# A layer norm over channel tiles with one mean product each, and the next stage's first weights prepared in it

## The chip, the cores and the metric
One core of a Trainium2 chip (trn2) runs the whole program: one launch, five engines (TensorE or PE, VectorE or DVE, ScalarE or ACT, GpSimd or POOL, and SyncE or SP, which issues transfers) and 16 DMA engines. The metric is the device time of one execution in microseconds, as the median of several runs.

## The reference
A layer of a diffusion backbone on 2048 tokens of 1024 channels, with 256 context tokens. What bears on the change:

```python
def conv_module(proj, taps, bias, ln_g, ln_b, conv_fn):
    u = proj[..., OFF_CONV_A:OFF_CONV_B] * jax.nn.sigmoid(proj[..., OFF_CONV_B:OFF_Q])
    u = conv_fn(u, taps) + bias
    return jax.nn.silu(layernorm(u, ln_g, ln_b))
...
def forget_gate(f_logits, lb):
    f = lb + (1.0 - lb) * jax.nn.sigmoid(f_logits.astype(jnp.float32))
    return split_heads(jnp.log(f)), split_heads(1.0 - f)
...
    lower_bounds = jnp.cumsum(jax.nn.softmax(hgrn_lb_logits, axis=0), axis=0)[:DEPTH]
```

One input projection (`w_in`, 3584 columns) feeds the convolution (columns A and B), the four heads of a gated recurrence (q, v, two forget gates FF and FB, output gate g). Convolution and heads are joined, projected out and gated; then comes a routed mixture of 16 experts, and a last norm.

## The kernel before, in words
The program is a row of stages, each with its own block of engine programs and its own scope `cleanup_on_exit`, which frees the stage's memory, clears its semaphores on GpSimd and ends in a barrier: `modulate_stage` (L96), `conv_stage` (L364), `heads_stage` (L739), `outproj_stage` (L1541), `topk_stage`, `moe_stage`. A further such scope, `front` (L2493), stands around the first two and holds `ConvWeights`, the four staging slabs `wst` for 128 columns of `w_in` each. Float32 weights are split into a bf16 high part (ScalarE casts) and a bf16 low part (VectorE subtracts), and every projection is three bf16 products (`triple`, L89 to L91), 24 instructions for a 512-token tile.

`conv_stage`. Channels lie on the partitions in four tiles (NCT = 4), tokens in four segments of 512 (NSEG = 4). PE makes the pairs A and B for each channel tile and segment (`pa`, `pb`, two banks each, with the semaphore `u_ok` giving the bank back); ScalarE takes the tanh (L506), VectorE the product `u` (`gated`, L579), then 31 taps per channel tile into `co` (L592, L607). POOL first issues the parameters (taps, bias `cb`, norm `lg`, then `adab`), and VectorE waits for `par_in` ahead of its first `gated` (L573).

Between its own work PE does *jobs* in a fixed order `KIND`: 18 for v, 32 for q and g, and four small ones, "mod", which sum the products of `modulation`. Each job is written to one of four PSUM banks `pjob`; ScalarE copies it into `jb` (L496, two buffers) and POOL stores it (L474). Twelve jobs lie beside the pairs, 17 beside the taps, and `LN_JOBS` spreads the others over the four segments of the layer norm, with the last two in `REST`.

The layer norm, for each segment n: PE multiplies `co` by a constant matrix of 1/512 for each of the four channel tiles into `pmu` (`mean`, L715); VectorE subtracts (`centre`, L625); ScalarE squares into one of two buffers `sq` (L525); PE multiplies each by the same matrix into `pva` (L728); ScalarE takes the root (L534), VectorE the reciprocal (L644) and scales (L648); then for each channel tile ScalarE scale and bias (L549), tanh (L552), VectorE the product (L659), ScalarE a bf16 cast (L541), VectorE the low part (L654), and SP stores both. After every second channel tile VectorE makes one `modulation` sum (L633, L636), eight instructions of 256 elements, from rows that SP has loaded into the place of `u`. `mean(n + 1)` is issued ahead of segment n's variance.

`heads_stage`. For each head, ten units of up to 512 tokens alternate in direction. A unit's gate: PE projects with `whi`, `wlo` (`project`, L1431), ScalarE takes the tanh (L1065), VectorE makes f with the constants `gh` and `gb` (L1237), POOL makes k = 1 - f (`keep`, L997), ScalarE the log, VectorE the running sum with `segm` (L1247), ScalarE the exponentials (L1081, L1083), POOL the decayed k into the block matrix `KX` and `KK` (`decay_k`, L1006 to L1013), PE its transposes (L1441), and so on. The stage starts with the loads of the norm's scale `ng` and the bound logits `lbr` (SP L902, L903, POOL L977), the first head's weights (L909), cast (L1057) and subtracted (L1225), and `lbd`, `gh`, `gb` (L1214 to L1218, L1052). POOL makes the masks `segm` and `msk` first, and clears `AT` and `KX` (L1029 to L1031) after two `keep`.

## Time and profile before

| what | value |
|---|---|
| median of 3 runs | 2456.59 us (2454.57 to 2457.14) |
| the profiled execution's own time | 2455.54 us |
| its span, first to last instruction | 2453.8 us |
| mean granted clock of TensorE | 0.957 of full speed |

The profile is of one execution. A row of the timeline is: start in us, duration in us, engine, line, operation, output tile <- input tiles, form, count, and in brackets the idle time of the engine before it with what ended it. PE rows of neighbouring matmuls overlap: each shows its whole way through the array, while the next starts before it ends. DMA rows on SP and POOL show the issue, not the transfer.

### The profile page before, as it was taken

The numbers are of one execution on the slowest core, as the hardware profiler recorded it, in microseconds if no ns is written. First come the engines' busy times: TensorE is split into PE (matmuls) and PEld (weight loads), VectorE is DVE, ScalarE is ACT, GpSimd is POOL, SyncE is SP. The second block draws the span as 40 slices with busy tenths as digits, with TensorE's granted clock in tenths as the row PEclk, the third lists the DMA queues.
The fourth block names the chain that finished last, engine by engine and source line by source line (L and its number), as shares of the span: only waits on it lengthen the run. The fifth ranks groups of instructions, "written<-read, shape, count | busy, mean of one in ns | idle before, by whom it ended". The sixth has DMA issues, their size and how long they took to land. (4 is left out here: it accounts for less than half of the span.)

```text
span 2453.8 us, 38986 instructions
## 1 busy us (share of the span) xinstructions
PE 2256.4 (92%) x14964; PEld 1514.2 (62%) x14964; DVE 1565.2 (64%) x2251; ACT 1039.6 (42%) x1333; POOL 547.9 (22%) x572
## 2 busy tenths in 40 slices
PE   7799999996999898979994699999999999999995
PEld 3344444433777786845552477777777777777773
DVE  2759998554668686843334566666666666666666
ACT  3511011443555656544442244444444444444445
POOL 1600001002546464603334111111110111111111
PEclk9799999998999999979996799999999999999998
DMA  8431013344011111334445376777667677676676
GB/s 325 83 78 35 18 30 109 97 142 127 8 48 42 48 41 30 119 104 151 144 155 210 129 240 218 230 234 230 225 220 231 217 234 225 221 239 226 220 248 257
DMA packets 220978, 379.51 MB, mean 155 GB/s; under 512 B 43970, under 2 KB 81986, under 8 KB 220363
## 3 DMA queue, kind: packets, MB, share of 16 engines
q1 hardware_dynamic: 202620, 319.22, 39.1%
q0 software_dynamic: 16656, 56.99, 8.6%
q10 hardware_dynamic: 1616, 2.16, 0.3%
q8 instruction: 53, 0.87, 0.2%
q14 instruction: 33, 0.27, 0.0%
HBM read 314.62 MB, written 63.72 MB: 154 GB/s over the span
## 5 line engine op out<-in xcount | busy, mean ns | idle before, releaser
L89 PE MATMUL pgu<-xhi,mwhi 128*128 128x256 bf16 x2048 | 559.6, 273 | 0.8 <-DVE xlo L2288 0.8
L91 PE MATMUL pgu<-xhi,mwlo 128*128 128x256 bf16 x2048 | 559.6, 273 | 0.0
L90 PE MATMUL pgu<-xlo,mwhi 128*128 128x256 bf16 x2048 | 559.5, 273 | 0.0
L2293 DVE TENSOR_TENSOR mwlo<-mwst,mwhi 128x2048 bf16<-128x2048 f32 x187 | 426.9, 2283 | 0.0
L2197 ACT ACTIVATE mwhi<-mwst 128x2048 bf16<-128x2048 f32 x186 | 350.8, 1902 | 0.0
L2205 ACT ACTIVATE thb<-pgu 128x256 f32<-128x256 f32 x128 | 49.1, 384 | 550.9 <-PE pgu L91 550.9
L607 DVE SCALAR_TENSOR_TENSOR co<-u,taps,co 128x1984 f32<-128x1984 f32 (+22 forms) x120 | 234.1, 1951 | 3.7
L2137 POOL TENSOR_TENSOR mpflag<-mpflag 1x1 f32<-1x1 f32 x46 | 37.2, 808 | 855.6 <-DVE ysb L2320 579.1
L2304 DVE SCALAR_TENSOR_TENSOR thb<-thb,pgu 128x256 f32<-128x256 f32 x128 | 53.8, 420 | 261.7 <-ACT thb L2205 261.7
L89 PEld LDWEIGHTS pgu<-xhi,mwhi 128*128 128x128 bf16 x2048 | 200.8, 98 | 26.1 <-DVE xlo L2288 1.1
L90 PEld LDWEIGHTS pgu<-xlo,mwhi 128*128 128x128 bf16 x2048 | 200.8, 98 | 24.9
L91 PEld LDWEIGHTS pgu<-xhi,mwlo 128*128 128x128 bf16 x2048 | 200.8, 98 | 23.6
L2445 PE MATMUL pd<-mwhi,fhi 128*128 128x512 bf16 x512 | 194.8, 381 | 4.2 <-DVE ysb L2320 3.0
L2447 PE MATMUL pd<-mwhi,flo 128*128 128x512 bf16 x512 | 194.7, 380 | 0.0
L2446 PE MATMUL pd<-mwlo,fhi 128*128 128x512 bf16 x512 | 194.7, 380 | 0.0
L1453 PEld LDWEIGHTS pat<-E,KX 128*128 128x128 f32 x1024 | 150.2, 194 | 23.3 <-POOL KX L1013 8.5
L1431 PE MATMUL pj<-hhi,hwhi 128*128 128x512 bf16 (+1 forms) x320 | 118.4, 370 | 46.1 <-DVE hwlo L1225 27.5
L1453 PE MATMUL pat<-E,KX 128*128 128x32 f32 x1024 | 143.8, 251 | 11.1 <-POOL KX L1013 6.3
L1431 PE MATMUL pj<-hlo,hwhi 128*128 128x512 bf16 (+1 forms) x320 | 118.1, 369 | 0.0
L1431 PE MATMUL pj<-hhi,hwlo 128*128 128x512 bf16 (+1 forms) x320 | 117.5, 367 | 0.0
L496 ACT ACTIVATE jb<-pjob 128x512 f32<-128x512 f32 (+1 forms) x54 | 31.6, 594 | 172.7 <-PE pjob L91 149.8
L2320 DVE SCALAR_TENSOR_TENSOR ysb<-pd,gate,g 128x512 f32<-128x512 f32 x64 | 47.9, 749 | 84.5 <-PE pd L2447 84.5
(352 smaller groups left out, 4426.9 us busy)
## 6 DMA issues: line engine op xcount, KB each, us to landing
mwst<-in_w_gate SPq DMA_DIRECT2D x32, 2048.0 KB, 8.9
mwst<-in_w_up SPq DMA_DIRECT2D x32, 2048.0 KB, 7.9
mwst<-in_w_down SPq DMA_DIRECT2D x32, 2048.0 KB, 7.9
big<-in_ada_w SPq DMA_DIRECT2D x5, 2048.0 KB, 13.1
wst<-in_w_in SPq DMA_DIRECT2D x20, 512.0 KB, 4.9
s_rows<-row SPq DMA_DIRECT2D x16, 520.0 KB, 2.9
u<-in_ada_w SPq DMA_DIRECT2D x8, 1024.0 KB, 6.4
xt<-in_x SPq DMA_DIRECT2D x16, 512.0 KB, 4.4
```

Of the source, the lines that this page charges most:

```text
L89: nc.tensor.matmul(out, lh, rh, start=(k == 0), stop=False)
L90: nc.tensor.matmul(out, lh, rl, start=False, stop=False)
L91: last = nc.tensor.matmul(out, ll, rh, start=False, stop=(k == n - 1))
L607: nc.vector.scalar_tensor_tensor(o, i, taps[:, c, k:k + 1], o, ALU.mult, ALU.add).then_inc(tap_ok, 1)
L1431: ins = nc.tensor.matmul(pj[:, 0:n], w, x, start=(mm == 0), stop=(mm == 3 * KD - 1))
L1453: ins = nc.tensor.matmul(pat[:, n * CH:(n + 1) * CH], KX[:, p, n * P:(n + 1) * P], E[:, p, n * CH:(n + 1) * CH], start=True, stop=True)
L2197: nc.scalar.activation(whi[:, b, ks], wst[:, b % NS, ks], ACT.Copy).then_inc(w_hi, 1)
L2293: nc.vector.tensor_tensor(wlo[:, b, ks], wst[:, b % NS, ks], whi[:, b, ks], ALU.subtract)\
L2304: nc.vector.scalar_tensor_tensor(thb[:, p], thb[:, p], 1.0, pgu[p][:, 0, :], ALU.add, ALU.mult)\
L2445: nc.tensor.matmul(pd[q % 2][:], fh, whi[:, 4 + c, k, :], start=(k == 0), stop=False)
L2446: nc.tensor.matmul(pd[q % 2][:], fh, wlo[:, 4 + c, k, :], start=False, stop=False)
L2447: last = nc.tensor.matmul(pd[q % 2][:], fl, whi[:, 4 + c, k, :], start=False, stop=(k == KD - 1))
```

## The change
It has three parts.

In the conv stage's layer norm VectorE sums the four channel tiles (`channel_sum`, into the free buffer `th`) and the four squares (`square_sum`, in `sq`, now four buffers), in two adds each, and PE makes one product for the mean and one for the variance. The order of jobs around them is new: one before `mean(n + 1)`, one before the variance; the "mod" job is second in its group. `modulation` has one buffer `msum` and other places in VectorE's order; PE's wait for all the taps goes. The squares of the next segment are made right after the root. The last three jobs are stored by SP, with semaphores `late_out` of their own.

A class `GateWeights`, allocated for the whole mixer, holds weights, parameters and bounds of the heads. It uses the four slabs of `wst` (two for staging, one each for high and low). The conv stage loads the first head's two weight blocks, casts and subtracts them in segment 0, queues the parameters on POOL behind the conv stage's, and makes `lbd`, `gh`, `gb`, `ng`. The scope `front` is gone; its tiles live in the mixer's scope.

The heads stage starts with `load(0)` on SP; its loads of `ng` and `lbr`, `load_w(0)`, and the first head's casts, subtractions and bounds are removed; POOL clears `KX[:, 0]` ahead of `msk`, VectorE clears `KX[:, 1]` and `AT` at its start.

```diff
+class GateWeights:
+    def __init__(self, m, I, st):
+        self.st = st[:, 0:2]
+        self.hi = st[:, 2].rearrange("p k n -> p (k n)").bitcast(BF16).rearrange("p (d k n) -> p d k n", d=2, k=KD)
+        self.lo = st[:, 3].rearrange("p k n -> p (k n)").bitcast(BF16).rearrange("p (d k n) -> p d k n", d=2, k=KD)
...
+    def load(self, sp, h, d):
+        col = (COL_FF, COL_FB)[d]
+        sp.dma_start(self.st[:, d], self.src[:, :, bass.ds(h * P + col, P)]).then_inc(self.loaded[d], 16)
...
-            KIND.insert(first + WITH_LN, ("mod", n - 1))
+            KIND.insert(first + 1, ("mod", n - 1))
-    KIND.append(("mod", NSEG - 1))
+    KIND.insert(-1, ("mod", NSEG - 1))
...
@@ SP, conv stage @@
                 load_ada(0)
                 load_ada(1)
+                sp.wait_ge(w_lo, len(SLAB))
+                for d in range(2):
+                    GW_.load(sp, 0, d)
                 for n in range(NSEG):
                     for c in range(NCT):
                         q = n * NCT + c
+                        if c in (0, 2) and n + 1 < NSEG:
+                            e = 2 * n + c // 2
+                            sp.wait_ge(ada_ok, KD * (e + 1))
+                            load_ada(e + 2)
                         sp.wait_ge(ml_ok, q + 1)
...
-                        if q % 2 == 1 and q // 2 + 2 < 2 * NSEG:
-                            sp.wait_ge(ada_ok, KD * (q // 2 + 1))
-                            load_ada(q // 2 + 2)
+                for j in LATE:
+                    sp.wait_ge(job_ok, j + 1)
+                    sp.dma_start(*to_store(j)).then_inc(late_out[j % 2], 16)
...
@@ POOL, conv stage, after adab @@
+                    pool.dma_start(GW_.ng[:], I["hgrn_norm_g"][0].rearrange("(h p) -> p h", p=P)).then_inc(GW_.par_in, 16)
+                    for l in range(2):
+                        for d in range(2):
+                            pool.dma_start(GW_.lbr[:, l, d, :], I["hgrn_lb_logits"][l, d].rearrange("(h p) -> p h", p=P))\
+                                .then_inc(GW_.par_in, 16)
...
@@ ScalarE, conv stage @@
+                nc.scalar.activation(GW_.lbd[:], GW_.lbd[:], ACT.Tanh, scale=0.5).then_inc(GW_.lb_ok, 1)
+                squares(0)
                 for n in range(NSEG):
...
+                    job(LN_JOBS[n][0])
+                    act.wait_ge(va_ps, n + 1)
...
                     job(LN_JOBS[n][1])
+                    if n + 1 < NSEG:
+                        squares(n + 1)
+                    job(LN_JOBS[n][2])
+                    if n == 0:
+                        for d in range(2):
+                            act.wait_ge(GW_.loaded[d], 16)
+                            nc.scalar.activation(GW_.hi[:, d], GW_.st[:, d], ACT.Copy).then_inc(GW_.hi_ok, 1)
...
@@ VectorE, conv stage @@
                 nc.vector.tensor_scalar(lg[:], lg[:], 0.5, None, ALU.mult).then_inc(par_ok, 1)
+                dve.wait_ge(GW_.par_in, 80)
+                nc.vector.tensor_tensor(GW_.lbd[:], GW_.lbr[:, 0], GW_.lbr[:, 1], ALU.subtract).then_inc(GW_.lb_ok, 1)
+                nc.vector.tensor_scalar(GW_.ng[:], GW_.ng[:], 0.5, None, ALU.mult).then_inc(GW_.lb_ok, 1)
...
+                def channel_sum(n):
+                    if n >= 1:
+                        dve.wait_ge(mu_ps, n)
+                    x = co[:, :, n * SEG:(n + 1) * SEG]
+                    nc.vector.tensor_tensor(th[:], x[:, 0:2], x[:, 2:4], ALU.add).then_inc(sx_ok, 1)
+                    dve.wait_ge(sx_ok, 2 * n + 1)
+                    nc.vector.tensor_tensor(th[:, 0], th[:, 0], th[:, 1], ALU.add).then_inc(sx_ok, 1)
+                def square_sum(n):
+                    dve.wait_ge(sq_ok, NCT * (n + 1))
+                    nc.vector.tensor_tensor(sq[:, 0:2], sq[:, 0:2], sq[:, 2:4], ALU.add).then_inc(ss_ok, 1)
+                    dve.wait_ge(ss_ok, 2 * n + 1)
+                    nc.vector.tensor_tensor(sq[:, 0], sq[:, 0], sq[:, 1], ALU.add).then_inc(ss_ok, 1)
...
+                channel_sum(0)
                 centre(0)
+                channel_sum(1)
+                square_sum(0)
...
                 for n in range(NSEG):
                     if n + 1 < NSEG:
                         centre(n + 1)
+                    if n + 2 < NSEG:
+                        channel_sum(n + 2)
+                    modulation(2 * n)
+                    if n == NSEG - 1:
+                        modulation(2 * n + 1)
...
+                    if n + 1 < NSEG:
+                        square_sum(n + 1)
...
-                        if c % 2 == 1:
-                            modulation(q // 2)
+                        if c == 1 and n < NSEG - 1:
+                            modulation(2 * n + 1)
                     low(n * NCT + NCT - 1)
+                    if n == 0:
+                        for d in range(2):
+                            dve.wait_ge(GW_.hi_ok, d + 1)
+                            nc.vector.tensor_tensor(GW_.lo[:, d], GW_.st[:, d], GW_.hi[:, d], ALU.subtract)\
+                                .then_inc(GW_.lo_ok, 1)
...
@@ PE, conv stage @@
-                pe.wait_ge(tap_ok, NCT * TAPS)
...
-                    for c in range(NCT):
-                        last = nc.tensor.matmul(pmu[n % 2][:], K["mean_cw"][:], co[:, c, n * SEG:(n + 1) * SEG],
+                    pe.wait_ge(sx_ok, 2 * n + 2)
+                    nc.tensor.matmul(pmu[n % 2][:], K["mean_cw"][:], th[:, 0], start=True, stop=True).then_inc(mu_ps, 1)
                 mean(0)
                 for n in range(NSEG):
+                    job(LN_JOBS[n][0])
                     if n + 1 < NSEG:
                         mean(n + 1)
+                    job(LN_JOBS[n][1])
...
+                    pe.wait_ge(ss_ok, 2 * n + 2)
+                    nc.tensor.matmul(pva[n % 2][:], K["mean_cw"][:], sq[:, 0], start=True, stop=True).then_inc(va_ps, 1)
+                    for j in LN_JOBS[n][2:]:
                         job(j)
...
@@ heads stage @@
-                load_w(0)
...
@@ POOL, heads stage @@
                 nc.gpsimd.memset(segm[:], 1.0).then_inc(msk_ok, 1)
+                nc.gpsimd.memset(pflag[:], 0.0).then_inc(pf_ok, 1)
+                wait(pool, msk_ok, 1)
+                nc.gpsimd.memset(segm[:, 0:SEG:P], 0.0).then_inc(msk_ok, 1)
+                nc.gpsimd.memset(KX[:, 0], 0.0).then_inc(zero_ok, 1)
                 nc.gpsimd.memset(msk[:], 1.0).then_inc(msk_ok, 1)
...
@@ VectorE, heads stage @@
-                wait(dve, msk_ok, 5)
+                nc.vector.memset(KX[:, 1], 0.0).then_inc(at0_ok, 1)
+                nc.vector.memset(AT[:], 0.0).then_inc(at0_ok, 1)
...
@@ build @@
-            with nc.cleanup_on_exit(), ExitStack() as front:
-                CW_ = ConvWeights(Mem(nc, front), I)
-                modulate_stage(nc, K, I, scr, CW_)
-                conv_stage(nc, K, I, scr, CW_)
+            CW_ = ConvWeights(mm, I)
+            GW_ = GateWeights(mm, I, CW_.st)
+            modulate_stage(nc, K, I, scr, CW_)
+            conv_stage(nc, K, I, scr, CW_, GW_)
```

## Rows read from the trace of the kernel before

**Rows 1.** The page: busy time of the engines.
```profile
PE 2256.4 (92%) x14964; PEld 1514.2 (62%) x14964; DVE 1565.2 (64%) x2251; ACT 1039.6 (42%) x1333; POOL 547.9 (22%) x572
```

**Rows 2.** Busy time by stretch: microseconds, engines (busy, count), PEclk, DMA share, GB/s.
```profile
120.00:431.00 311.00, 311.00 (x1442) 141.05 (x1441) 266.40 (x158) 41.52 (x60) 22.78 (x32) 1.00 0.20 56
431.00:581.00 150.00, 145.61 (x586) 61.38 (x584) 82.92 (x132) 67.28 (x102) 13.51 (x26) 1.00 0.37 110
581.00:600.00 19.00, 0.39 (x2) 0.28 (x3) 2.37 (x10) 2.10 (x3) 5.50 (x10) 0.53 0.52 137
```

**Rows 3.** Timeline, first PE matmul of heads: start, us, idle before.
```profile
599.62 0.39 PE L1431 MATMUL pj<-hhi,hwhi 128*128 128x256 bf16 x1 [19.54 <-DVE hwlo L1225]
```

**Rows 4.** Groups by line, 431 to 581 us: count, busy us, mean ns, idle before.
```profile
L728 PE MATMUL pb<-sq,mean_cw 128*128 128x512 f32 x32 | 16.2, 609 | 3.5 <-ACT sq L525 3.5
...
L715 PE MATMUL pa<-co,mean_cw 128*128 128x512 f32 x32 | 14.3, 596 | 0.0
L644 DVE RECIPROCAL rs<-rs 128x512 f32<-128x512 f32 x4 | 13.4, 3353 | 34.0 <-ACT rs L534 34.0
...
L659 DVE SCALAR_TENSOR_TENSOR y<-tl,y 128x512 f32<-128x512 f32 x16 | 11.0, 690 | 16.1 <-ACT tl L552 16.1
```

**Rows 5.** Timeline in the layer norm, ACT, PE and VectorE.
```profile
426.07 0.60 ACT L496 ACTIVATE jb<-pjob 128x512 f32<-128x512 f32 x1 [4.58 <-PE pjob L91]
...
431.05 7.03 PE L715 MATMUL pa<-co,mean_cw 128*128 128x512 f32 x16
...
434.76 2.48 DVE L625 TENSOR_TENSOR co<-co,pa 128x512 f32<-128x512 f32 x4 [12.92 <-PE pa L715]
...
492.14 3.61 DVE L636 SCALAR_TENSOR_TENSOR msum<-u,sil,msum 128x256 f32<-128x256 f32 x7
```

**Rows 6.** Timeline at the end of the conv stage, PE, POOL and SP.
```profile
579.06 1.01 PE L683 MATMUL pjob<-adab,ident 4*1 4x512 f32 x2
...
580.99 0.51 POOL L474 DMA_DIRECT2D s_modrows<-jb  x1 [1.30 <-ACT jb L496]
...
588.87 0.39 SPq L902 DMA_DIRECT2D ng<-in_hgrn_norm_g  x1
```

**Rows 7.** Timeline of the parameters of the conv stage, POOL, VectorE, ScalarE.
```profile
129.08 0.78 POOL L458 DMA_DIRECT2D cb<-in_conv_bias  x1 [12.96 <-issue]
...
130.59 0.75 POOL L460 DMA_DIRECT2D lg<-in_conv_ln_b  x1
...
133.21 0.23 DVE L573 TENSOR_SCALAR taps<-taps 128x124 f32<-128x124 f32 x1 [18.83 <-DMA lg<-in_conv_ln_b]
...
134.01 1.22 DVE L568 TENSOR_TENSOR wlo<-wst,whi 128x1024 bf16<-128x1024 f32 x1
...
136.00 0.60 ACT L506 ACTIVATE th<-pb 128x512 f32<-128x512 f32 x1 [7.37 <-PE pb L91]
```

**Rows 8.** Stores: issues by tile with median us to landing; SP's timeline.
```profile
s_modrows<-jb POOLq DMA_DIRECT2D x1, 2.0 KB, 1.6
...
s_mixed<-ml SPq DMA_DIRECT2D x5, 128.0 KB, 2.0
...
1070.51 2.09 SPq L964 DMA_DIRECT2D s_mixed<-KX  x4
1075.63 0.56 SPq L1608 DMA_DIRECT2D hhi<-s_mixed  x1
```

**Rows 9.** Timeline of the first units of the heads stage, POOL, VectorE, PE.
```profile
611.45 1.79 POOL L1031 MEMSET KX<- 128x2048 f32 x1
613.33 1.01 POOL L1006 TENSOR_TENSOR KX<-KK,B 128x256 f32<-128x256 f32 x1
...
610.68 2.59 DVE L1254 COPY sm<-B 128x8 f32<-128x8 f32 x1
...
615.09 0.44 PE L1441 MATMUL pk<-ident,KK 128*128 128x128 f32 x2 [1.83 <-POOL KK L1009]
```

More of the change, by code:

```diff
@@ L899, in _ @@
             def _(sp):
-                with nc.allow_non_contiguous_dma(reason="per-channel constants into columns"):
-                    sp.dma_start(ng[:], I["hgrn_norm_g"][0].rearrange("(h p) -> p h", p=P)).then_inc(m_out[0], 16)
-                    sp.dma_start(lbr[:, 0, 0, :], I["hgrn_lb_logits"][0, 0].rearrange("(h p) -> p h", p=P))\
-                        .then_inc(m_out[1], 16)
                 def load_w(h):
-                    for d, col in enumerate((COL_FF, COL_FB)):
+                    for d in range(2):
                         wait(sp, w_lo, h * 2 - 1 + d)
-                        sp.dma_start(wst[:, d], wv[:, :, bass.ds(h * P + col, P)]).then_inc(w_in[d], 16)
+                        GW_.load(sp, h, d)
                 def load(h):
@@ L1049, in _ @@
             def _(act):
-                wait(act, lb_ok, 1)
-                nc.scalar.activation(lbd[:], lbd[:], ACT.Tanh, scale=0.5).then_inc(lb_ok, 1)
                 def split(h, d):
@@ L1349, in _ @@
                     constants(0, d)
[L1350 removed]
                 forget(0, 0)
+                wait(dve, msk_ok, 2)
                 sums(0, 0)
```

168 lines of the change are left out of this document (70 added, 98 removed).

## The prediction

> **What bounds the kernel now.** I read the page first, for the shares of the engines; then the busy time of each engine in chosen stretches; then TensorE's waits and the groups of instructions in the layer norm; last the timeline at the places that the diff touches.
>
> TensorE is busy for 92% of the span [rows 1]. The stretches say more [rows 2]. From 120 to 431 us (projections on PE, the taps on VectorE) PE is busy for all of the 311 us: a microsecond taken from or added to PE is one of the kernel, and VectorE only has to deliver in time. From 431 to 581 us (the layer norm, with q and g projections between) PE has 145.61 of 150 us, VectorE 82.92, ScalarE 67.28: again PE. From 581 to 600 us PE has 0.39 us of work: one stage ends and the next starts, and nothing hides it. The largest wait of PE there is for `hwlo`, the low half of the first head's gate weights, 19.5 us at a time [rows 3]. Nothing behind the heads stage is touched, so what is won ahead of it should reach the end whole.
>
> I measure against the profiled execution: 2455.54 us, span 2453.8 us. The median of the runs shown is 2456.59 us, 1.05 us above it; I add that at the end. 0.2%, 4.9 us, is about what a measurement of this kernel can tell from no change.
>
> **Part 1: the mean products.** Before, each segment has four float32 products for the mean and four for the variance, two instructions each: 32 on L715 and 32 on L728 [rows 4]. The first 16 run in 7.03 us, the last one's drain of 0.6 included, so one starts every 0.43 us [rows 5]. The change leaves a quarter, 16 instructions. PE loses 48 x 0.43 = 20.6 us.
>
> With them go stalls. PE's stretch of the layer norm runs from 430.8 us (just ahead of the first L715, [rows 5]) to 580.07 us (the end of the last L683, [rows 6]): 149.2 us. By the code it holds 21 projection jobs; their pitch is that between two of ScalarE's copies, 4.58 idle + 0.60 = 5.18 us [rows 5], together 108.8. Four modulation jobs are two pairs of instructions, 1.0 us each pair [rows 6]: 8.0. The 64 products: 27.5. The rest, 149.2 - 144.3 = 4.9 us, is waiting; 3.5 us of it are for the squares [rows 4]. Afterwards a job stands between each product and what it needs, so I let 1 us remain: 3.9 us gained. Bounds: none, or all 4.9.
>
> Does VectorE keep up? A middle segment holds: the centring, 2.48; the modulation sums twice, 3.61 for seven instructions of eight, so 4.0 each [rows 5]; the reciprocal, 3.35 [rows 4]; four scalings of the centring's form, 2.5; four of L659 and four splits of the same size at 0.69 [rows 4], 5.5. That is 21.8 us. New are two pairs of adds. The first add of a pair has 1024 elements and two inputs; the nearest row is the 1024-element subtraction of 1.22 us [rows 7]; the second has 512, 0.68. Two pairs: 3.8 us, together 25.6 us. Of the waits for the tanh 16.1 us over 16 stay, 4 us a segment at most [rows 4]; the sums cover some, I allow 3. So VectorE needs 28.6 us a segment and PE 5 x 5.18 + 2.0 + 4 x 0.43 = 29.6 us. It is close, but PE stays the bound, and VectorE starts ahead: it idles 12.92 us until the first mean [rows 5]. In the last segment both modulation sums come ahead of the reciprocal, 8 us, but centring and channel adds are gone there; by this count VectorE ends some 8 us before PE. The second modulation sum of a segment is needed by the second job of the next; walking both queues it is there about 4 us early each time. ScalarE has slack of half the stretch. The stores of the last three jobs move from POOL to SP, behind the `mixed` stores, which are out when VectorE ends. `load_ada` moves ahead of a store on SP and comes earlier.
>
> **Part 2: the parameters.** The norm's scale and the logits, five transfers of 512 four-byte elements, are now queued on POOL at the start of the conv stage, behind `adab`, and VectorE waits for all of them ahead of its first `gated`. POOL issues `cb` and `lg` 0.75 us apart, the last `lg` at 130.59; it has landed at 133.2 us, 2.6 us later, when VectorE starts [rows 7]. With `adab` and five more at 0.75 the last issue is at 135.1 us, landed at 137.7. With 0.2 us of small operations and 0.68 for L579, the first `u` is there at 138.6 us. PE needs it for its third pair of products; ScalarE's tanh of the second comes at 136.00 us [rows 7], and PE's first instruction of the third would be 0.2 us ahead of that. Cost: 138.6 - 135.8 = 2.8 us, on the path, since PE has no idle time from there on. Behind VectorE's wait are the splits of the slabs, which nobody needs so soon. Bounds: nothing, or a landing twice as long, 5.4 us.
>
> PE's end of the stage: 580.07 - 20.6 - 3.9 + 2.8 = 558.4 us.
>
> **Part 3: the end of the stage.** Before, the last store is issued at 580.99, lands 1.6 us later, and SP's first instruction of the next stage is at 588.87, 6.3 us after that [rows 6, 8]. Two clean-ups stand in that gap, of the conv stage and of the scope `front`; the change takes the second away. From the heads to the output projection there is one: the last of four stores is issued at 1072.1 us, lands 2 us later, and the next stage begins at 1075.63 [rows 8], a gap of 1.5 us. So a clean-up is worth nothing to 4.8 us. I take a gap of 3.0 us, nearer to the boundary with the same number. The last store is now of 256 KB on SP instead of 2 KB: SP's of 128 KB land in 2.0 us [rows 8]; I take 2.5, bounds 2 and 4. Next stage: 558.4 + 0.9 + 2.5 + 3.0 = 564.8 us, 24.1 us earlier.
>
> **Part 4: the first head's weights.** Before, PE's first product comes at 599.62 us, 10.75 us after SP's first instruction [rows 3, 6]: load, cast, subtraction. These now stand in the conv stage: two loads on SP while it has nothing else, two casts on ScalarE, two subtractions of 1.22 us [rows 7] on VectorE in the first segment, covered by its lead; without the lead they would cost 2.4 us. PE starts about 0.7 us after SP: gain 10.0 us.
>
> **Part 5: the memsets.** Before, POOL clears `AT` and `KX` between `keep` and `decay_k`; the last takes 1.79 us and `decay_k` starts when it ends, at 613.33 [rows 9]. Now POOL clears half of `KX` ahead and VectorE the rest, while PE projects its first 24 products: POOL has 1.8 us for `KX` and, by that rate, 1.4 for the two others, and the masks, some 5 us, about what PE, ScalarE and VectorE need before `keep`. What PE gains is not the memsets' time but its own wait for `KK`, 1.83 us [rows 9]; next late is PE's own third projection, which ends then. Gain 1.8 us, bounds 0 and 4.
>
> VectorE's copy into `sm` took 2.59 us here, ending with POOL's last memset [rows 9]. The Trainium skill ("SBUF — State Buffer", its part on which ports contend) says that VectorE and GpSimd share a port pair by an exclusive lock held for a whole instruction; the trace agrees. If VectorE's new memsets took that lock too, which no row shows, POOL would be done some 3 us later: part 5 would be worth nothing, its lower bound.
>
> **The sum.** 24.1 + 10.0 + 1.8 = 35.9 us. 2455.54 - 35.9 = 2419.6 us; for the median 2420.7 us.
>
> **The rivals.**
> (a) The gap keeps its 6.3 us, because the start of this stage costs it and not the second clean-up. Against: the boundary at 1075 us. 2420.7 + 3.3 = 2424.0 us. Chance 15%.
> (b) VectorE becomes the bound of the layer norm. For it: 1 us of slack in a segment. With the adds or waits 2 us longer PE waits for sums or variances, 4 to 8 us in all: 2425 to 2429 us. Against: VectorE's lead. Chance 12%.
> (c) POOL's queue stalls once more. It idled 12.96 us ahead of `cb` [rows 7], behind the taps. If the added transfers meet that limit once, the parameters come 13 us later, and PE stands: 2434 us. Against: three of the same size went out 0.75 us apart. Chance 5%.
> (d) Slower, at the same place: every added transfer meets the stall, 5 x 12.96 = 65 us, and PE, without cover, loses it: 2486 us. It decides from the point where the last logits land 36 us later than I say, after 173 us. Chance 2%.
> (e) The change doesn't do what it says: the wait at 599 us comes back as another, for `v`, `q` or the masks, and 10 us less are gained: 2431 us. Against: the first product with `v` comes behind the transposes, which start at 615.09 us [rows 9]. Chance 4%.
>
> **How the numbers follow.** The forecast gets 62%, with a range of its own from 2414 to 2425 us: below, a clean-up worth 1.5 us more, no delay of the parameters (2.8), all stalls gone (1); above, 4 us of terms lost. (a) and (b) reach to 2429 us; so the range is 2412 to 2430 us and leaves out (c), (d), (e) and a rest. Faster by over 0.2%: 0.97, all but (d) and a rest; within 0.01; slower 0.02.
>
> **What would show it.** L715 and L728 with eight instructions each; VectorE's first `u` at 138.6 us; PE's layer norm about 124.7 us long instead of 149.2 and 2.8 us later in its start; 5.5 us from the last store's issue to the next stage, and PE's first product within 1 us of it; no wait for `KK` at the first transposes. PE waits of over 4 us for sums in the layer norm, a pause near 136 us of over 6 us, or a next stage that starts after 570 us would prove me wrong.

## The result and the profile after

The changed kernel takes 2415.24 us, the median of 4 runs (2414.21 to 2418.06), beside 2456.86 us for the kernel before on the same chip: a ratio of 0.9833, with a 95% interval of 0.9816 to 0.9850. The forecast was 2420.7 us in a range of 2412 to 2430. The gain by medians is 41.6 us; between the two profiled executions it is 2453.8 - 2411.7 = 42.1 us of span, where the steps of the forecast add up to 35.9. So the direction and the places were right and 6.2 us are to be accounted for.

The page of the changed kernel, busy time of the engines, beside [rows 1]:

```profile
PE 2220.3 (92%) x14770; PEld 1503.6 (62%) x14916; DVE 1578.7 (65%) x2269; ACT 1038.9 (43%) x1333; POOL 544.5 (23%) x569
```

The weight loads (PEld) are 48 fewer, the number of products taken out; PE's own count is 194 lower, so some 146 of its records are missing here, and its 36.1 us less must not be read as work saved. The stretches below and the timeline are the surer guide. VectorE has 13.5 us more. Busy time by stretch, changed kernel (columns as in [rows 2]):

```profile
120.00:430.80 310.80, 308.06 (x1413) 139.99 (x1432) 268.38 (x162) 41.45 (x60) 26.45 (x37) 1.00 0.20 55
430.80:555.00 124.20, 123.67 (x528) 52.65 (x536) 97.98 (x150) 68.14 (x104) 12.37 (x23) 1.00 0.47 139
555.00:560.00 5.00, 0.76 (x6) 0.57 (x6) 0.23 (x1) 0.60 (x1) 0.70 (x4) 0.97 0.14 53
```

The layer norm is a stretch of 124 us in which PE stands still for half a microsecond; the 19 us of nothing between the stages, 581 to 600 before, are 4.2 us. New is the first line: PE lacks 2.7 us of 310.8 (a part of it missing records), where it had lacked none.

Groups by line in the layer norm, 430.8 to 555 us, changed kernel (columns as in [rows 4]):

```profile
L717 DVE RECIPROCAL rs<-rs 128x512 f32<-128x512 f32 x4 | 13.4, 3348 | 1.3 <-ACT rs L572 1.3
...
L734 DVE SCALAR_TENSOR_TENSOR y<-tl,y 128x512 f32<-128x512 f32 x16 | 10.9, 690 | 10.6 <-ACT tl L597 10.6
...
L679 DVE TENSOR_TENSOR sq<-sq 128x1024 f32<-128x1024 f32 x4 | 4.9, 1219 | 0.0
L805 PE MATMUL pb<-sq,mean_cw 128*128 128x512 f32 x8 | 4.4, 631 | 0.0
L794 PE MATMUL pa<-th,mean_cw 128*128 128x512 f32 x8 | 4.1, 592 | 0.0
...
L673 DVE TENSOR_TENSOR th<-co 128x1024 f32<-128x1024 f32 x3 | 3.7, 1218 | 0.0
```

32 and 32 product instructions are 8 and 8, and neither waits any more (L728 waited 3.5 us before [rows 4]). An add of 1024 elements takes 1.22 us, the row that the forecast took for it; VectorE's wait of 34.0 us for the root [rows 4] is 1.3 us, since the order of the work gives it something else to do meanwhile.

The timeline of the parameters, changed kernel, POOL's and then VectorE's and PE's rows:

```profile
126.38 0.78 POOL L499 DMA_DIRECT2D cb<-in_conv_bias  x1 [11.91 <-issue]
...
129.18 0.80 POOL L504 DMA_DIRECT2D ng<-in_hgrn_norm_g  x1
129.95 3.00 POOL L507 DMA_DIRECT2D lbr<-in_hgrn_lb_logits  x4
...
131.45 0.23 DVE L618 TENSOR_SCALAR taps<-taps 128x124 f32<-128x124 f32 x1 [18.71 <-DMA lg<-in_conv_ln_b]
...
134.83 0.17 DVE L621 TENSOR_TENSOR lbd<-lbr 128x8 f32<-128x8 f32 x1 [3.07 <-DMA lbr<-in_hgrn_lb_logits]
...
135.72 0.39 PE L89 MATMUL pa<-hhi,whi 128*128 128x512 bf16 x1 [1.64 <-DVE u L627]
```

The five transfers go out some 0.75 us apart and no second stall of POOL follows them: rivals (c) and (d) did not come. VectorE waits 3.07 us for the logits, and PE then 1.64 us for VectorE. The cost is read against the first product of the convolution, and in this profile its record is missing, as the weight loads show (the first PE record is of L90, the second product):

```profile
110.52 0.10 PEld L89 LDWEIGHTS pa<-hhi,whi 128*128 128x128 bf16 x1 [8.93 <-DVE wlo L613]
...
110.93 0.63 PE L90 MATMUL pa<-hlo,whi 128*128 128x512 bf16 x1 [9.09 <-DVE wlo L613]
```

So the first product started at 110.53 us, where it was 112.16 before. From there the first mean product comes 318.89 us later before and 320.46 after: the parameters cost 1.6 us, the length of the pause.

The timeline at the end of the conv stage, changed kernel: VectorE's last instruction, ScalarE, SP and the next stage's first rows (beside [rows 3, 6, 9]):

```profile
549.85 0.69 DVE L729 TENSOR_TENSOR ml<-y,mh 128x512 bf16<-128x512 f32 x1 [0.45 <-ACT mh L586]
...
549.73 1.07 ACT L535 ACTIVATE jb<-pjob 128x512 f32<-128x512 f32 x2
553.88 0.59 ACT L535 ACTIVATE jb<-pjob 1x512 f32<-1x512 f32 x1 [3.09 <-DMA s_g<-jb]
555.11 0.60 ACT L535 ACTIVATE jb<-pjob 128x512 f32<-128x512 f32 x1 [0.64 <-PE pjob L91]
...
555.73 0.36 SPq L487 DMA_DIRECT2D s_g<-jb  x1
559.27 0.35 SPq L978 DMA_DIRECT2D v<-s_v  x1
...
559.31 0.27 PE L1472 MATMUL pj<-hhi,wst 128*128 128x256 bf16 x1 [4.24 <-PEq L406]
...
559.77 1.76 DVE L1260 MEMSET KX<- 128x2048 f32 x1 [9.23 <-PEq L406]
559.89 1.81 POOL L1038 MEMSET KX<- 128x2048 f32 x1
...
572.92 0.38 PE L1482 MATMUL pk<-ident,KK 128*128 128x128 f32 x2
```

From the last store's issue to the next stage 3.54 us pass, where it was 7.88 [rows 6]; PE's first product comes 0.04 us behind SP's first instruction, where it was 10.75; and the transposes at 572.92 us wait for nothing, where they waited 1.83 us [rows 9].

### The profile page after: what moved, and what is told of

Same layout as the page of the kernel before. It is cut to its first block and busy times, and to the rows that moved or that the text cites. A ratio compares the mean times of both kernels' runs of the same rounds, so it can differ in the third digit from the quotient of the medians.

```text
span 2411.7 us, 38747 instructions
## 1 busy us (share of the span) xinstructions
PE 2220.3 (92%) x14770; PEld 1503.6 (62%) x14916; DVE 1578.7 (65%) x2269; ACT 1038.9 (43%) x1333; POOL 544.5 (23%) x569
## 5 line engine op out<-in xcount | busy, mean ns | idle before, releaser
L90 PE MATMUL pgu<-xlo,mwhi 128*128 128x256 bf16 x2048 | 559.1, 273 | 0.0
L1472 PE MATMUL pj<-hhi,wst 128*128 128x512 bf16 (+1 forms) x606 | 210.3, 370 | 28.9 <-ACT G L1116 16.2
L90 PEld LDWEIGHTS pgu<-xlo,mwhi 128*128 128x128 bf16 x2048 | 200.7, 98 | 24.8
L2487 PE MATMUL pd<-mwlo,fhi 128*128 128x512 bf16 x497 | 189.1, 381 | 2.9 <-DVE flo L2353 1.4
L2486 PE MATMUL pd<-mwhi,fhi 128*128 128x512 bf16 x481 | 182.9, 380 | 3.3 <-DVE ysb L2361 3.0
L1472 PEld LDWEIGHTS pj<-hhi,wst 128*128 128x128 bf16 x640 | 82.7, 129 | 52.5 <-issue 25.1
L1472 PE MATMUL pj<-hlo,wst 128*128 128x512 bf16 (+1 forms) x310 | 114.2, 368 | 0.9 <-ACT G L1116 0.9
L89 PE MATMUL pjob<-hhi,whi 128*128 128x512 bf16 x251 | 95.1, 379 | 0.3
```

The costliest lines, as they stand in the source:

```text
L89: nc.tensor.matmul(out, lh, rh, start=(k == 0), stop=False)
L90: nc.tensor.matmul(out, lh, rl, start=False, stop=False)
L1472: ins = nc.tensor.matmul(pj[:, 0:n], w, x, start=(mm == 0), stop=(mm == 3 * KD - 1))
L2486: nc.tensor.matmul(pd[q % 2][:], fh, whi[:, 4 + c, k, :], start=(k == 0), stop=False)
L2487: nc.tensor.matmul(pd[q % 2][:], fh, wlo[:, 4 + c, k, :], start=False, stop=False)
```

## The experiments

One execution of a kernel differs from the next by some us (2413.16 to 2417.81 for the changed kernel in after_again), so where a kernel ran once I compare stages of its trace and not its total. These are the marks, all in us. *Taps*: from the convolution's first product to the first mean product. In five profiles (before_again, changed, pool_last and the two with `tail` in the name) the record of that first product is missing; there I count from 0.40 us ahead of the second, the distance that the other nine show. *Norm*: from there to ScalarE's last copy of a job, less the 0.04 us between a job's end and its copy; PE does the whole of it without a pause, unless said. *Gap*: from the last store's issue to SP's first instruction of the heads stage. *First*: from there to PE's first product. *Transposes*: from that product to the first transposes.

| kernel | median (runs) | taps | norm | gap | first | transposes |
|---|---|---|---|---|---|---|
| before | 2456.86 (4) | 318.9 | 149.0 | 7.9 | 10.75 | 15.5 |
| changed | 2415.24 (4) | 320.5 | 124.1 | 3.5 | 0.04 | 13.6 |
| before_again | 2453.48 (1) | 318.6 | 149.3 | 7.9 | 10.7 | 15.2 |
| after_again | 2415.50 (5) | 322.5 | 124.1 | 3.5 | 0.04 | 14.3 |
| scope | 2416.52 (1) | 320.7 | 124.1 | 3.9 | 0.04 | 13.5 |
| pool_last | 2421.27 (1) | 320.7 | 124.1 | 8.3 | 0.04 | 14.5 |
| weights_back | 2422.74 (1) | 322.6 | 124.1 | 3.5 | 6.2 | 14.5 |
| four | 2435.31 (1) | 320.6 | 144.7 | 3.5 | 0.04 | 13.6 |
| memsets | 2417.73 (1) | 320.6 | 124.1 | 3.5 | 0.04 | 15.6 |
| late_par | 2414.15 (5) | 318.9 | 124.1 | 3.5 | 0.04 | 14.4 |
| vector_3us | 2420.30 (1) | 320.4 | 130.4 | 3.5 | 0.05 | 13.9 |
| vector_7us | 2433.95 (1) | 320.6 | 144.0 | 3.5 | 0.04 | 14.0 |
| vector_3us_tail | 2423.78 (1) | 323.1 | 128.0 | 4.8 | 0.04 | 13.4 |
| late_par_tail | 2414.75 (5) | 318.6 | 124.1 | 3.5 | 0.04 | 14.5 |

**Both kernels once more, unchanged**, for how far a profile can be trusted.

> The kernel before once more. Five profiles of the changed kernel and its variants have PE's first product of the conv stage at 110.3 to 112.3 us, the one of before has it at 112.16. If the stage ahead merely strays, this one lies in the same band and PE's first product to the first mean product is 318.9 us again; the gap from the last store's issue to the heads stage is again near 7.9 us.

> The changed kernel once more, to see how far one execution's stages stray. The forecast and the trace differ by 6.2 us: 1.6 us lie ahead of the conv stage, in code that is the same. If that is a matter of the execution, this profile puts PE's first product of the conv stage anywhere between 110.9 and 112.2 us and the rest of the stages keep their lengths to 0.3 us. If the change does it, it comes at 110.9 us again. Median near 2415 us.

The ratio of after_again is 0.9838 (0.9824 to 0.9851). Norm and gap repeat within 0.3 us in both kernels. What does not repeat is the beginning: the convolution's first product comes between 110.3 and 112.3 us in all the profiles, whatever the kernel (110.33 in after_again, outside the band that I expected), and the taps in the changed kernel took 320.5 us in one execution and 322.5 in the other. The second of these has its reason in late_par, below.

**scope: a second clean-up around the first two stages again.**

```diff
-            modulate_stage(nc, K, I, scr, CW_)
-            conv_stage(nc, K, I, scr, CW_, GW_)
+            with nc.cleanup_on_exit():
+                for i in range(4):
+                    nc.alloc_semaphore(f"spare{i}")
+                modulate_stage(nc, K, I, scr, CW_)
+                conv_stage(nc, K, I, scr, CW_, GW_)
```

> Changed kernel with a second clean-up scope around the first two stages, with four semaphores in it, as the kernel before had. Theory A (the second clean-up is what made the gap long): from the last store's issue to SP's first instruction of the heads stage 3.5 us becomes some 8 us, and the span grows by 4 to 5 us. Theory B (rival a: something in the start of this stage cost it): the gap stays within 0.5 us of 3.5 us and the span as it is.

SP's timeline in scope:

```profile
556.52 0.36 SPq L487 DMA_DIRECT2D s_g<-jb  x1
560.45 0.35 SPq L978 DMA_DIRECT2D v<-s_v  x1
```

The gap is 3.93 us against 3.54. A second clean-up with its barrier costs 0.4 us here, where SP issues the last stores. The forecast had given it 3.3 of the 6.3 us, so the gap had another cause, and there was one more thing that the change had altered there: which queue issues the last three stores.

**pool_last: the last three jobs stored by POOL again.**

```diff
-                for j in LATE:
-                    sp.wait_ge(job_ok, j + 1)
-                    sp.dma_start(*to_store(j)).then_inc(late_out[j % 2], 16)
...
-                for j in range(LATE[0]):
+                for j in range(JOBS):
```

> Changed kernel with the last three jobs stored by POOL, as before the change, and not by SP. The run with a second clean-up scope had a gap of 3.93 us against 3.54, so the scope is worth 0.4 us and the 4.4 us by which the gap fell are open. Theory A (it is the stores: POOL's last store, with its clean-up behind it on the same engine, holds the barrier): the gap from the last store's issue to SP's first instruction of heads is 7 to 8 us and the span 4 us longer. Theory B (it is what else went from the boundary): 3.5 us plus 0.7 for a slower landing at most.

Timeline of SP and of POOL at the end of the stage, pool_last:

```profile
564.82 0.36 SPq L971 DMA_DIRECT2D v<-s_v  x1
...
556.51 0.56 POOL L506 DMA_DIRECT2D s_g<-jb  x1 [0.79 <-ACT jb L528]
564.82 0.52 POOL L1027 MEMSET segm<- 128x512 f32 x1 [7.75 <-POOLq L406]
```

A gap of 8.3 us with a single clean-up. The store itself is hardly slower: it lands 2.7 us after its issue, SP's last one in the changed kernel after 2.4 us. So 5.6 us lie between the landing and the next stage where POOL has issued the last store and 1.1 us where SP has. In the kernel before, with POOL's store and two clean-ups, they were 6.3 us, so with POOL as the issuer too the second clean-up is worth at most 0.7 us. What POOL does in the 5.6 us no row shows; its idle time is put down to its own sequencer. The Trainium skill ("DMA: Bandwidth & Descriptors", its first table) gives a transfer from GpSimd about 1 us to its first byte and one from SyncE 0.6 us. By that estimate the store would cost 0.4 us more from POOL; the run says 4.8 us, only 0.3 of it on the way to memory.

**weights_back: loads, casts and subtractions of the first head's weights in the heads stage again**, its bounds and parameters left in the conv stage.

```diff
-                sp.wait_ge(w_lo, len(SLAB))
-                for d in range(2):
-                    GW_.load(sp, 0, d)
...
+                load_w(0)
                 load(0)
...
+                split(0, 0)
+                split(0, 1)
                 gate(0, 0)
```

> Changed kernel, but the first head's weights are loaded, cast and subtracted at the start of the heads stage as before; bounds and parameters stay in the conv stage. Theory A (the chain load, cast, subtraction is the whole 10.7 us): PE's first product of heads comes 9 to 10.5 us after SP's first instruction, and the span grows by 8.5 to 10.5 us. Theory B (the parameters' transfers and the masks cost part of it): only 6 us or less. The layer norm should be the same length, 124.3 us, since the two casts and subtractions it loses had cover.

Timeline of ScalarE, VectorE and PE at the start of the heads stage, weights_back:

```profile
565.32 1.06 ACT L1097 ACTIVATE wst<-wst 128x1024 bf16<-128x1024 f32 x1 [7.38 <-DMA wst<-in_w_in]
...
566.40 1.23 DVE L1256 TENSOR_TENSOR wst<-wst 128x1024 bf16<-128x1024 f32 x1 [1.53 <-ACT wst L1097]
...
567.69 0.40 PE L1464 MATMUL pj<-hhi,wst 128*128 128x256 bf16 x1 [10.38 <-DVE wst L1256]
```

PE starts 6.2 us after SP, not 10.75. The kernel before shows where the other 4.5 us came from; its VectorE and ScalarE at the same place:

```profile
596.95 0.17 DVE L1214 TENSOR_TENSOR lbd<-lbr 128x8 f32<-128x8 f32 x1 [23.00 <-DMA lbr<-in_hgrn_lb_logits]
...
597.15 0.21 ACT L1052 ACTIVATE lbd<-lbd 128x8 f32<-128x8 f32 x1 [16.45 <-DVE lbd L1214]
597.26 1.99 ACT L1057 ACTIVATE hwhi<-hwst 128x1024 bf16<-128x1024 f32 x2
```

The casts stood in ScalarE's queue behind the tanh of `lbd`, which waited for the logits. Their three transfers from POOL, 2 KB each, took 3.3, 4.6 and 6.0 us to land beside the loads of weights, v and q. The first weights were there sooner: issued at 589.86 us, behind SP's two small transfers, landed 4.7 us later at 594.6, and cast from 597.26 only. In weights_back SP issues them at once, they land in 3.8 us, and the cast starts with the landing. So the 4.5 us are some 1.0 of SP's two issues, 0.9 of slower landing and 2.7 of waiting for the logits. This follows from the rows of the two traces; moving the parameters alone was not tried.

**four: four products for each mean and variance again**, VectorE's adds out, the new order of jobs and all else kept.

```diff
-                    pe.wait_ge(sx_ok, 2 * n + 2)
-                    nc.tensor.matmul(pmu[n % 2][:], K["mean_cw"][:], th[:, 0], start=True, stop=True).then_inc(mu_ps, 1)
+                    pe.wait_ge(tap_ok, NCT * TAPS)
+                    for c in range(NCT):
+                        last = nc.tensor.matmul(pmu[n % 2][:], K["mean_cw"][:], co[:, c, n * SEG:(n + 1) * SEG],
+                                                start=(c == 0), stop=(c == NCT - 1))
+                    last.then_inc(mu_ps, 1)
...
-                channel_sum(0)
                 centre(0)
-                channel_sum(1)
-                square_sum(0)
```

> Changed kernel with the four products for the mean and four for the variance put back and VectorE's adds taken out; the new order of jobs stays. Theory A (my sum: the products cost 0.43 us an instruction, the rest was waiting that the new order takes away): PE's layer norm is 124.3 + 20.6 = 144.9 us long, against 149.2 us of the kernel before; so the new order alone is worth 4.3 us and the adds the rest. Theory B (the adds also took the waiting away): 149 us, as before.

Groups by line, four, 430 to 577 us (columns as in [rows 4]):

```profile
L802 PE MATMUL pb<-sq,mean_cw 128*128 128x512 f32 x32 | 14.7, 602 | 0.0
L788 PE MATMUL pa<-co,mean_cw 128*128 128x512 f32 x32 | 14.4, 592 | 0.0
```

The norm takes 144.7 us: 144.7 - 124.1 = 20.6 us for 48 product instructions, 0.43 us each, as read from the row of 16. The rest of the gain, 149.0 - 144.7 = 4.3 us, belongs to what this run kept: the order of the jobs, the squares made earlier and their four buffers, which no run takes apart. The products wait for nothing here either. And VectorE's adds, 8 x 1.22 + 8 x 0.69 = 15.3 us of its time, cost nothing.

**memsets: AT and KX cleared by POOL behind the two `keep` again.**

```diff
-                nc.gpsimd.memset(KX[:, 0], 0.0).then_inc(zero_ok, 1)
                 nc.gpsimd.memset(msk[:], 1.0).then_inc(msk_ok, 1)
...
                 keep(0, 1)
+                nc.gpsimd.memset(AT[:], 0.0).then_inc(zero_ok, 1)
+                nc.gpsimd.memset(KX[:, 1], 0.0).then_inc(zero_ok, 1)
+                nc.gpsimd.memset(KX[:, 0], 0.0).then_inc(zero_ok, 1)
...
-                nc.vector.memset(KX[:, 1], 0.0).then_inc(at0_ok, 1)
-                nc.vector.memset(AT[:], 0.0).then_inc(at0_ok, 1)
```

> Changed kernel with POOL clearing AT and KX between keep and decay_k again, VectorE none. Theory A (part 5 of the forecast): PE waits some 1.8 us for KK at the first transposes, and the span grows by 1.5 to 2 us. Theory B (the memsets were hidden): no wait and no change.

Timeline of POOL, VectorE and PE in memsets:

```profile
572.95 1.79 POOL L1087 MEMSET KX<- 128x2048 f32 x1
572.18 2.60 DVE L1293 COPY sm<-B 128x8 f32<-128x8 f32 x1
...
576.59 0.44 PE L1481 MATMUL pk<-ident,KK 128*128 128x128 f32 x2 [1.83 <-POOL KK L1065]
```

The wait of 1.83 us is back to the digit, and VectorE's copy takes 2.60 us again, ending with POOL's memset; in the changed kernel the same copy of 8 elements takes 0.17 us. Counted from PE's first product the transposes come 15.6 us later, 2.0 us more than in the changed kernel's first profile. Over all the profiles that keep the new memsets this mark lies between 13.4 and 14.5 us (the table), and it goes with the granted clock of the 5 us from PE's first product on: 13.4 us at 0.70, 13.6 at 0.66 (twice), 13.9 at 0.59, 14.5 at 0.50. In memsets that clock is 0.66, so the 13.6 us are the right measure and the memsets are worth 2.0 us, near the wait.

**late_par: VectorE's wait for the logits moved to the end of the taps**, the transfers where they are.

```diff
@@ VectorE, conv stage @@
-                dve.wait_ge(GW_.par_in, 80)
-                nc.vector.tensor_tensor(GW_.lbd[:], GW_.lbr[:, 0], GW_.lbr[:, 1], ALU.subtract).then_inc(GW_.lb_ok, 1)
-                nc.vector.tensor_scalar(GW_.ng[:], GW_.ng[:], 0.5, None, ALU.mult).then_inc(GW_.lb_ok, 1)
...
                 dve.wait_ge(tap_ok, steps)
+                dve.wait_ge(GW_.par_in, 80)
+                nc.vector.tensor_tensor(GW_.lbd[:], GW_.lbr[:, 0], GW_.lbr[:, 1], ALU.subtract).then_inc(GW_.lb_ok, 1)
+                nc.vector.tensor_scalar(GW_.ng[:], GW_.ng[:], 0.5, None, ALU.mult).then_inc(GW_.lb_ok, 1)
@@ ScalarE, conv stage @@
+                act.wait_ge(GW_.lb_ok, 2)
                 nc.scalar.activation(GW_.lbd[:], GW_.lbd[:], ACT.Tanh, scale=0.5).then_inc(GW_.lb_ok, 1)
```

> Changed kernel, but VectorE waits for the logits and makes lbd and ng only after the taps, not ahead of its first gated product. Theory A (the parameters stand on PE's path): the 1.64 us pause of PE at 134 us goes, and the layer norm starts and the kernel ends 1.6 us earlier than the changed kernel, about 2413.5 us. Theory B (the pause is absorbed later, where PE waits anyway): the same time as the changed kernel, with a new wait elsewhere.

The taps take 318.9 us, as before the change and 1.6 us less than in the changed kernel's first profile, and PE has no pause. Busy time from 130 to 140 us (columns as in [rows 2]), in late_par, and in a second fence in after_again, the changed kernel's other execution:

```profile
130.00:140.00 10.00, 10.00 (x48) 4.51 (x47) 3.94 (x6) 1.54 (x2) 4.85 (x7) 1.00 0.39 65
```

```profile
130.00:140.00 10.00, 7.91 (x30) 3.06 (x29) 4.01 (x8) 1.54 (x2) 3.17 (x5) 0.83 0.32 54
```

In after_again PE stands 2.09 us at this place, and the granted clock of these 10 us is 0.83: a part of them ran at 1.2 GHz instead of 2.4. Its taps cost 322.5 - 318.9 = 3.6 us more than late_par's, the pause and 1.5 us of slower products. The profile first shown had a pause of 1.64 us and a clock of 1.00 there, and cost 1.6. So one wait has two prices. Of the ten profiles with this pause, seven have one of 1.57 to 1.81 us and a clock of 1.00; three have a longer one and the lower clock (this one, weights_back with 2.15 us and 0.83, vector_3us_tail with 2.69 us and 0.86). The pause follows the stall of POOL ahead of `cb`, which is there without the change too: 11.9 to 12.2 us in the seven, and 12.32, 12.43 and 13.12 us in the three. What makes the stall longer in some executions stays open. The time of late_par is 2414.15 us (2413.11 to 2415.01), ratio 0.9833 (0.9819 to 0.9846). The changed kernel ran from 2413.16 to 2417.81 on the same chip; the intervals overlap, so the 1.6 us are in the stage and not proven in the total.

**vector_3us and vector_7us: one and two reciprocals more on VectorE in each segment**, 3.35 us each, whose result nobody reads.

```diff
+                    dve.wait_ge(sx_ok, 2 * min(n + 3, NSEG))
+                    for i in range(1):
+                        dve.wait_ge(jk_ok, 1 * n + i)
+                        nc.vector.reciprocal(th[:, 1], K["hhi"][:, 0, 0:SEG]).then_inc(jk_ok, 1)
                     modulation(2 * n)
```

(vector_7us has two of them.)

> Changed kernel with one more reciprocal of 512 elements (3.35 us, result not used) on VectorE in each segment, ahead of its first modulation sum. Theory A (VectorE's slack is what the trace shows at PE's mod jobs: 4.6, 5.1 and 7.4 us): PE waits 1 to 2 us in the second segment and the stage ends 1 to 3 us later. Theory B (rival b, VectorE is already as good as the bound): 3.35 us a segment are paid in full, 10 to 13 us.

> The same with two more reciprocals a segment, 6.7 us. By theory A the lead is used up: VectorE ends the layer norm after PE, 15 to 19 us later than in the changed kernel. If PE's length were still within 5 us of 124.3 us, VectorE's slack would be far larger than the trace says.

Of 4 x 3.35 = 13.4 us added the norm shows 6.3, more than the 1 to 3 expected; of 26.8 it shows 19.9, just above the 15 to 19. So about 7 us are free, and what is added behind them counts nearly once. The delay has three parts, which PE's last product of the stage tells apart: PE's waits, slower products behind a wait, and a last copy that starts late.

| part, us | vector_3us | vector_7us |
|---|---|---|
| PE waits for sums, for ScalarE | 0.7, 1.9 | 7.4, 1.5 |
| slower products and a small rest | 2.0 | 4.7 |
| last copy behind PE's end | 1.7 | 6.4 |

In vector_7us one wait for a sum is of 6.2 us: there VectorE is the bound inside the norm too, rival (b) made on purpose. The slower products of vector_3us follow its wait of 1.9 us for ScalarE. Busy time from 500 to 510 us (columns as in [rows 2]), in vector_3us and then in vector_3us_tail (below), where a wait of the same length (2.17 us by the profile, which lacks the record of the first product behind it, so 1.95) is followed by the full clock:

```profile
500.00:510.00 10.00, 8.84 (x34) 3.70 (x35) 9.30 (x14) 4.95 (x8) 1.65 (x4) 0.83 0.74 231
```

```profile
500.00:510.00 10.00, 7.83 (x31) 2.94 (x31) 7.89 (x9) 3.89 (x7) 1.07 (x2) 1.00 0.82 235
```

The 36 products behind that wait take 9.25 us in the first and 7.55 in the second, so 1.7 of the 6.3 us are the clock of this one execution. The timeline of VectorE, ScalarE, SP and PE at the end of the stage, vector_3us:

```profile
556.28 0.69 DVE L734 TENSOR_TENSOR ml<-y,mh 128x512 bf16<-128x512 f32 x1 [0.45 <-ACT mh L587]
...
556.16 1.07 ACT L536 ACTIVATE jb<-pjob 128x512 f32<-128x512 f32 x2
560.30 0.59 ACT L536 ACTIVATE jb<-pjob 1x512 f32<-1x512 f32 x1 [3.07 <-DMA s_g<-jb]
561.51 0.60 ACT L536 ACTIVATE jb<-pjob 128x512 f32<-128x512 f32 x1 [0.63 <-DMA s_g<-jb]
...
558.00 0.54 SPq L488 DMA_DIRECT2D s_g<-jb  x1
...
565.73 0.37 PE L1477 MATMUL pj<-hhi,wst 128*128 128x256 bf16 x1 [5.96 <-PEq L406]
```

PE has ended at 565.73 - 5.96 = 559.77 us, and the last copy starts at 561.51, 5.2 us after the start of VectorE's last instruction. In the changed kernel it is the same distance (549.85 to 555.11), though there the copy waits for PE. The forecast counted "some 8 us" from VectorE's end to PE's; the changed kernel shows 4.5 us (550.54 to 555.07). And ScalarE copies the last jobs only behind its last cast, the copy in front needs one of two buffers back, and the store that gives it back stands on SP behind the `mixed` stores: a chain of 5.2 us from VectorE's last instruction on. In the changed kernel that store is issued at 551.57 and lands 3.4 us later, at 555.0, where PE ends at 555.07. So in the changed kernel this chain is within about 0.1 us of being the bound.

**vector_3us_tail and late_par_tail: two of the last four jobs copied earlier in ScalarE's order**, beside its work for channel tiles 2 and 3 of the last segment, and only the last two stores on SP; once on vector_3us, once on late_par.

```diff
-        LATE = range(JOBS - 3, JOBS)
+        LATE = range(JOBS - 2, JOBS)
...
+                        if n == NSEG - 1 and c >= 2:
+                            job(LN_JOBS[n][c + 2])
-                    for j in LN_JOBS[n][4:]:
+                    for j in LN_JOBS[n][4:] if n < NSEG - 1 else ():
```

> The run with one more reciprocal a segment cost 6.3 us, while PE waited only 2.6 us for it. Theory A (the tail: ScalarE's copies of the last jobs stand behind its last casts, and the last copy waits for a store that SP has queued behind the mixed stores): with those copies made between the casts and one more job stored by POOL, the layer norm is 126.7 to 127.3 us long instead of 130.4. Theory B (VectorE's added time is paid through PE all along): 130 us as without the edit.

> Changed kernel with both edits: parameters awaited after the taps, and the last copies between the casts. No extra work. By the trace the tail hides just behind PE in the changed kernel (0.6 us), so the second edit gives nothing by itself: the time is that of late_par, 2413 to 2415 us, with less spread than the changed kernel (2413.2 to 2417.8 us).

With the slowed VectorE the norm is 2.4 us shorter (130.4 to 128.0), less than the 3.1 to 3.7 foreseen, and the edit did not do most of that: 1.7 us are the products that kept the full clock in this execution, and the last copy starts 1.0 us behind PE's end instead of 1.7. The gap took it back, 4.8 us for 3.5. The end of the stage, POOL and SP, vector_3us_tail:

```profile
559.15 0.54 POOL L512 DMA_DIRECT2D s_g<-jb  x1 [2.34 <-ACT jb L536]
...
562.89 0.37 SPq L488 DMA_DIRECT2D s_g<-jb  x1
567.64 0.35 SPq L985 DMA_DIRECT2D v<-s_v  x1
```

POOL's last store is now 3.7 us ahead of SP's, where it was 5.1 in vector_3us. It lands after 3.0 us, and the next stage starts 5.5 us behind that, nearly as in pool_last (5.6), and 2.3 us behind the landing of SP's, where 1.1 is usual. So by these two runs it is not enough that the very last store is SP's: POOL's own last one must also be out some 8.5 us before the next stage can start. The total is no comparison: this execution's taps took 323.1 us. Where PE is the bound the edit brings nothing: the norm keeps 124.1 us, the time is 2414.75 us (2414.01 to 2415.85), ratio 0.983 (0.9816 to 0.9843). Its heads stage began 1.8 us earlier than that of the profile first shown (557.49 against 559.27) and took 478.3 us to the output projection where the other took 474.4: a difference that no part of the edit touches and that is larger than what I was looking for. 0.8 us of it lies ahead of the first transposes, the clock that memsets told of; the rest stays open. Neither version can be told from the changed kernel by its total; late_par is the simpler and takes the one new wait away.

## Why the prediction was right, and where it was not

| term, gain in us | forecast | measured |
|---|---|---|
| start of the conv stage | 0 | 1.6 |
| parameters | -2.8 | -1.6 |
| products | 20.6 | 20.6 (four) |
| stalls of PE in the norm | 3.9 | 4.3 (four) |
| PE's end to the next stage | 2.4 | 4.6 |
| PE's first product | 10.0 | 10.7 |
| transposes | 1.8 | 1.9 |
| sum | 35.9 | 42.1 |

The measured column is read from the two profiles, with the norm's 24.9 us split by the run four.

**Part 1, the products**, was right in the terms of its sum: 0.43 us an instruction, adds that PE never sees, 1.22 us for the first add. Its ledger of the norm, 21 jobs, four modulation jobs and the products, gives 108.8 + 8.0 + 6.9 = 123.7 us for the changed kernel, and the stretch takes 124.3 us. The 4.9 us of waiting that it found as a remainder were there; 0.6 us stay instead of 1. Rival (b), VectorE as the bound, did not come, but the step "VectorE ends some 8 us before PE" was wrong twice: it ended 4.5 us before, and what follows VectorE's end must be counted too. Its last instruction started 5.2 us before the last copy, and 5.2 us are what the chain behind it takes.

**Part 2, the parameters**: the mechanism was right, the size was not: 1.6 us for 2.8. The landing held (from the last issue, at 129.95 + 3 x 0.75 = 132.2, to 134.83 us: 2.6 us, as forecast), but POOL came to these transfers 2.7 us earlier than before (`cb` at 126.38 against 129.08 [rows 7]). 1.6 us of it is the earlier start of the stage, which moves PE's products as well and so changes nothing; 1.05 us is the shorter stall ahead of `cb`, 11.91 us for 12.96, and 2.8 - 1.05 = 1.75 us is nearly the pause. The forecast took the stall from one execution, the second longest of the fourteen. A fair figure is 1.6 to 3.6 us, as the changed kernel's two profiles show, because slower products can follow the pause. One moved wait avoids all of it (late_par).

**Part 3, the boundary**, is the step that was wrong: "a clean-up is worth nothing to 4.8 us. I take a gap of 3.0 us, nearer to the boundary with the same number." The two boundaries in the trace differed in the number of clean-ups and in the queue of the last stores [rows 6, 8], and I put the whole difference down to the first. The clean-up is worth 0.4 us (scope), the queue 4.8 us (pool_last). That a gain of this kind came at all is luck: it came because the change also moved the last stores to SP. With the clean-up gone and the stores left on POOL the gap is 8.3 us, where the forecast had 5.5 (2.5 and 3.0). I took the time behind the landing as 3.0 us and it was 1.1, near the 1.5 of the boundary at 1075 us, whose last stores are SP's too; that is 1.9 of the 2.2 us by which this term was short. The landing, 2.5 us forecast and 2.4 measured, was not at fault. Rival (a), "the start of this stage costs it", was wrong too: it was the end of the last one.

**Part 4, the first head's weights**: the gain was right within 0.7 us and the chain misnamed. "Load, cast, subtraction" is 6.2 us (weights_back). The other 4.5 us were the parameters: 2.7 us of waiting for the logits ahead of the casts, 1.0 of their issues ahead of the loads, 0.9 of slower loads. By these rows, moving the weights alone would have left the wait for the logits in place; no run tried it. What takes the place of the wait, rival (e), is nothing: the transposes came 42.2 us earlier (615.09 to 572.92), the whole gain.

**Part 5, the memsets**: 1.8 us forecast, 1.9 measured, 2.0 by the run. The doubt drawn from the Trainium skill ("SBUF — State Buffer", on which ports contend) is settled by two rows of the changed kernel: VectorE's memset from 559.77 us took 1.76 us beside POOL's of the same size from 559.89 with 1.81, so the two did not lock each other out. The same part of the page names as lockers, on VectorE's side, instructions in a two-port mode and ones with two inputs in SBUF, these against a GpSimd instruction that reads there; the copy of 2.60 us in memsets ended with POOL's memset, as one that was locked out would, and no row shows in which mode it ran.

**The start** has nothing to do with the change: before_again began at 110.56 us, 1.6 us earlier than the execution that I measured against, as the changed kernel did. A forecast from a single profile carries this, and here it fell on the side of the gain.

## What to carry to other kernels

When two boundaries between stages differ, list everything in which they differ before one of the differences gets the price; here the queue of the last stores cost 4.8 us and the clean-up 0.4. The slack of an engine ends with the last work that follows from it, not with its own last instruction: slowing the engine on purpose, in two sizes, showed 7 us and where they end. When such a run costs more than expected, look at the granted clock of its stretches before the cause gets a name: 1.7 of 6.3 us were the clock of one execution. And a wait put ahead of the bounding engine's supplier, though it measures 1.6 us, cost 3.6 us in an execution where it was 2.1 us long and slower products followed: put it where the supplier has a lead.

## What the runs showed of the hardware

With GpSimd as the issuer of the last store, 5.6 us lay between its landing and the next stage's first instruction, against 1.1 us with SyncE, though the stores of 256 KB landed in 2.7 and 2.4 us. Four transfers of 2 KB in four-byte elements took GpSimd 3.0 us to issue and landed after 2.5 to 2.7 us; three like them in the kernel before, beside large loads, after 3.3 to 6.0 us. TensorE's granted clock fell to 0.83 over 10 us around a pause of 2.1 us, and stayed at 1.00 around one of 1.64 us; around a pause of 1.9 us it was 0.83 in one execution (vector_3us) and 1.00 in another (vector_3us_tail), so the length of the pause alone does not decide it. A VectorE copy of 8 elements took 0.17 us, and 2.60 us when it met a GpSimd memset of 1.8 us, while a VectorE memset beside a GpSimd memset kept its time.
